# A stick-breaking attention loop: one copy moved from ScalarE to VectorE, four conditioning tiles and two column sums moved to later chunks

## The chip, the cores and the metric

The kernel runs on one NeuronCore of a Trainium2 chip. The metric is the device time of one execution in microseconds (us); lower is better.

## The reference, cut to what matters

Two layers with D_MODEL 2048, a sequence of 256 tokens, 16 heads of 128, and D_FF 8192. Layer 0 mixes tokens by stick-breaking attention, layer 1 by a short convolution; each is followed by a squared-ReLU MLP. Shift, scale and gate vectors come from a conditioning vector c through a product with mod_w, 2048 x 12288 per layer.

```python
mod = (cond @ mod_w[i] + mod_b[i])[:, None, :]
sh_m, sc_m, g_m, sh_f, sc_f, g_f = jnp.split(mod, N_MOD, axis=-1)
h = x * (1.0 + sc_m) + sh_m
# attention, each head:
z = jnp.einsum('bqhd,bkhd->bhqk', qb, kb) * scale
log_beta = jax.nn.log_sigmoid(z)
log_1m = jnp.where(causal, jax.nn.log_sigmoid(-z), 0.0)
log_stick = lax.cumsum(log_1m, axis=3, reverse=True) - log_1m
a = jnp.where(causal, jnp.exp(log_beta + log_stick), 0.0)
outs.append(jnp.einsum('bhqk,bkhd->bqhd', a, vb))
...
return o @ w_o
x = layer_norm(DEEPNORM_ALPHA * x + (1.0 + g_m) * y, ln_g[i, 0], ln_b[i, 0])
```

## The kernel before

**Weight products.** Each float32 operand is split into a rounded "high" part and the remainder, "low", and TensorE adds three products (high x high, high x low, low x high; L1215 to L1217). Weights go through in numbered chunks of 128 x 1024 elements. SyncE loads a chunk into one of eight places of `raw`; ScalarE writes `w_high` (L559), which has four slots; VectorE writes `w_low` (L872) and with it tells TensorE and the loader that the chunk is there and that its place is free. ScalarE may start on chunk n+4 when TensorE is through chunk n. So ScalarE's copy for chunk n+3 starts when chunk n begins on TensorE, where it isn't held up otherwise. A group is eight chunks, which fill two PSUM banks (128 tokens each). The chunks of the value projection are 64 to 95, those of the output projection W_O are 96 to 127; 96 to 99 are split before the attention loop.

**The conditioning vectors.** Their weights come as tiles of 128 x 1024. VectorE multiplies and adds each into `mod_acc` (L830; the first tile of a block of 16 is L827), through a ring of five buffers. When the 16 tiles of a block are done, TensorE sums over the partitions (`sum_mod`: eight transposes, L1241, or four matmuls for a gate, L1235) behind the chunk that SUMS_AFTER names, and VectorE takes the sums in (`write_block`, L838 and L861) in the step that WRITE_AFTER names. `step(n)` on VectorE is: `low(n)`, then a write if one is due, then the tiles of this step. All engine queues run in program order.

**The attention loop.** For head s: TensorE makes scores (L1350, L1352); ScalarE takes Abs, Exp and Ln (L630 to L634); VectorE makes the softplus (`sp`, L916); GpSimd masks it (L455, written to `stage`); TensorE adds running sums to the scores (`sums`, L1359 to L1361); ScalarE takes Exp (`probs`, L661); GpSimd masks that (L455); TensorE makes the output (L1371, L1373) in one of two PSUM tiles. Each engine's step s has a fixed order. TensorE: scores(s), sums(s-2), output(s-3). ScalarE: the three functions of head s, the Exp of head s-2, and `output_high(s-4)`, which copies a head's output to `h_high` (L652). VectorE: softplus(s), the tiles of this step, then the low part of output s-4 (L935). GpSimd: mask of softplus s, mask of probs s-2. TensorE's output(o) waits until the low part of output o-2 is written. The last two heads' sums and outputs run between the first chunks of W_O.

**The end of W_O.** `last_group` runs chunks 120 to 123 over both halves of the tokens, with a column sum behind a chunk where one is named, then chunks 124 to 127 over the first half, then the same four over the second. VectorE's part is this:

```python
                for j in range(SLOTS, NCH):
                    step(last + j)
                    if j == SLOTS:
                        take_both(n, NG - 2)
                take(n, NG - 1, 0)
```

Here `last` is 120; `take` adds a finished bank of the group to the residual rows (`take_both` both halves), and step 125 stands behind step 124 and `take_both`.

Of the kernel before, what the change touches and what calls it, by code (L numbers as in the profile page):

```python
# [23 lines left out]
ACT = mybir.ActivationFunctionType  # L24
# [4 lines left out]
CREDIT_BANKS = 2  # L29
# [5 lines left out]
def build_trunk(nc, x, c, mod_w, mod_b, ln_g, ln_b, attn_w_qkv, attn_w_o,  # L35
# [4 lines left out]
    KT = D // P  # L40
    TT = T // P
    HEADS = KT
    GC = 512
    GT = GC // P
    NCH = 8
# [13 lines left out]
    W_O = W_V + NG  # L59
# [19 lines left out]
    BANK0 = PARTS - 2 * NG  # L79
# [22 lines left out]
    def block_of(unit, half=HALVES - 1):  # L102
        return STARTS + HALVES * UNIT_ORDER.index(unit) + half
# [22 lines left out]
    N_V, N_O, N_HEADS, N_MLP0 = W_V * NCH, W_O * NCH, W_O * NCH + SLOTS, W_MLP[0] * NCH  # L126
# [4 lines left out]
    def start_chunk(p, jj):  # L131
        return LEADING * jj + p if p < LEADING else PART_CH * p + jj

    HEAD_TILES = {s: 1 for s in range(3, 16)} | {16: 2, 17: 2, 18: 2, 19: 1}
    N_HEAD_TILES = sum(HEAD_TILES.values())
    HEADS_BLOCK, HEADS_SUM, HEADS_WRITE = 8, 12, 14
    SUMS_AFTER = {12: 2, 27: 3, 42: 4, 58: 5, 74: 6, 90: 7, N_HEADS + 3: 9, N_HEADS + 20: 10}
    WRITE_AFTER = {14: 2, 30: 3, 45: 4, 62: 5, 78: 6, 94: 7, N_HEADS + 7: 9, N_HEADS + 24: 10}

    def tiles_early(n):  # L140
        if n < QC - 2:
            return 2 if n >= FIRST_STEP else 0
        if n < N_O:
            return 2 if n in (QC + 8, 2 * QC + 8) else 1
        return int(n < N_HEADS + 20)

    H_HIGH_ORDER = [(0, 0), (0, 1), (0, 2), (1, 0), (1, 1), (1, 2), (0, 3), (1, 3)]
    H_LOW_ORDER = [(0, 0), (0, 1), (1, 0), (0, 2), (1, 1), (1, 2), (0, 3), (1, 3)]
# [8 lines left out]
    done = TILES_FIRST + N_HEAD_TILES + sum(TILES_OF)  # L157
    for n0, n1, unit in ((N_MLP0 + 8, W_TAIL[1] * NCH + 20, UNITS + SHIFT_F),
                         (W_CIN * NCH + 8, W_COUT * NCH + 20, UNITS + SCALE_F),
                         (W_MLP[1] * NCH + 12, W_MLP[1] * NCH + 160, UNITS + GATE_F)):  # L160
        first, last, free = done, block_of(unit) * KT, 0
        TILES_OF += [0] * (n0 - len(TILES_OF))
        while done < last:
            n, now = len(TILES_OF), 0
            wanted = first + (n - n0 + 1) * (last - first) / (n1 - n0)
            while n >= free and done + now < min(wanted, last) and now < 2:
                now += 1
                if (done + now) % KT == 0:
                    SUMS_AFTER[n], WRITE_AFTER[n + 4], free = (done + now) // KT, (done + now) // KT, n + 4
            TILES_OF.append(now)  # L170
            done += now
    TILES_OF += [0] * (N_CHUNKS - len(TILES_OF))
# [14 lines left out]
    with ctx:  # L187
        def sb(name, shape, dt=F32):
            return ctx.enter_context(nc.sbuf_tensor(name, shape, dt))

        def sem(name):
            return ctx.enter_context(nc.semaphore(name))
# [15 lines left out]
        h_high = sb("h_high", [P, KT, T], F32R)  # L208
# [33 lines left out]
        o_ps = [bank[2][:, 0:T], bank[3][:, 0:T]]  # L242
# [18 lines left out]
        LEAD = 3  # L261
        STEPS = HEADS + 3
# [14 lines left out]
        banks_free = sem("banks_free")  # L277
# [23 lines left out]
        att_a, att_am, att_o = sem("att_a"), sem("att_am"), sem("att_o")  # L301
        att_hi, att_lo = sem("att_hi"), sem("att_lo")
# [196 lines left out]
        def _(act):  # L499
# [10 lines left out]
            for b, parts in enumerate(batches):  # L510
                row = 0 if b else KT
                for part in parts:
                    n = part.shape[0]
# [111 lines left out]
            def soft_log(s):  # L625
                e = soft[s % 2]
                act.wait_ge(att_z, s + 1)
                if s >= 2:
                    act.wait_ge(att_sp, s - 1)
                act.activation(e, z_ps[s % 4][:, 0:ZC], ACT.Abs).then_inc(att_act, 1)  # L630
                act.wait_ge(att_act, 2 * s + 1)
                act.activation(e, e, ACT.Exp, scale=-1.0).then_inc(att_act, 1)
                act.wait_ge(att_act, 2 * s + 2)
                act.activation(e, e, ACT.Ln, bias=1.0).then_inc(att_l, 1)  # L634
# [12 lines left out]
                    act.wait_ge(chunk_mult, W_O * NCH + CREDIT_SPLIT)  # L647
                empty(g % 2, lambda b: v_tok[:, b, g * GC:(g + 1) * GC])

            def output_high(o):  # L650
                act.wait_ge(att_o, o + 1)
                act.activation(h_high[:, o, :], o_ps[o % 2], ACT.Copy).then_inc(att_hi, 1)  # L652

            for s in range(2, HEADS + 2):
                if LEAD <= s < HEADS:
                    soft_log(s)
                a = s - 2
                act.wait_ge(att_cum, a + 1)
                if a >= 3:
                    act.wait_ge(att_o, a - 2)  # L660
                act.activation(probs[:, a % 3, :], z_ps[a % 4][:, 0:ZC], ACT.Exp).then_inc(att_a, 1)  # L661
                if s >= 4:
                    output_high(s - 4)
            for o in range(HEADS - 2, HEADS):
                output_high(o)

            def make_h(n, t, q):

# [121 lines left out]
        def _(dve):  # L790
# [79 lines left out]
            def low(n):  # L870
                dve.wait_ge(high_done, n + 1)
                dve.tensor_tensor(w_low[:, n % SLOTS], raw[:, n % NCH], w_high[:, n % SLOTS].bitcast(F32),  # L872
                                  ALU.subtract).then_inc(raw_used, 1)

            def step(n):

                low(n)
                if n in WRITE_AFTER:
                    write_block(WRITE_AFTER[n])
                add_tiles(TILE_AT[n], TILE_AT[n] + TILES_OF[n])  # L880
# [31 lines left out]
            def softplus(s):  # L912
                dve.wait_ge(att_l, s + 1)
                if s >= 3:
                    dve.wait_ge(att_cum, s - 2)
                dve.scalar_tensor_tensor(out=sp[s % 3], in0=z_ps[s % 4][:, 0:ZC], scalar=0.0,  # L916
                                         in1=soft[s % 2], op0=ALU.max, op1=ALU.add).then_inc(att_sp, 1)
# [3 lines left out]
            head_tile = TILE_AT[N_HEADS] - N_HEAD_TILES  # L921


            for s in range(LEAD, STEPS + 1):
                if s < HEADS:
                    softplus(s)
                if s == HEADS_WRITE:
                    write_block(HEADS_BLOCK)
                add_tiles(head_tile, head_tile + HEAD_TILES.get(s, 0))
                head_tile += HEAD_TILES.get(s, 0)  # L930
                o = s - 4
                if o < 0:
                    continue
                dve.wait_ge(att_hi, o + 1)
                dve.tensor_tensor(h_low[:, o, :], o_ps[o % 2], h_high[:, o, :].bitcast(F32),  # L935
                                  ALU.subtract).then_inc(att_lo, 1)
# [218 lines left out]
            n = LNS - 1  # L1155
# [17 lines left out]
        def _(pe):  # L1173
# [55 lines left out]
            def sum_mod(b):  # L1229

                pe.wait_ge(mod_chain, block_chained(b))
                acc = mod_acc[:, b % 2, :]
                if is_gate(b):
                    for i in range(2):
                        ins = pe.matmul(gate_ps[i][:, :], ones[:], acc[:, cols(i)], start=True, stop=True)  # L1235
                elif b > 1:
                    if b == 2:
                        pe.wait_ge(turned_out, 2 + TT * NG)
                    for t in range(WT):
                        dst = turned_sums(b)[t // GT][:, t % GT * P:(t % GT + 1) * P]  # L1240
                        ins = pe.transpose(dst, acc[:, t * P:(t + 1) * P], ident[:])  # L1241
                else:
                    for t in range(WT // 2):
                        ins = pe.matmul(mod_ps[:, t:t + 1], acc[:, t * P:(t + 1) * P], ones[:, 0:1],
                                        start=True, stop=True)
                ins.then_inc(mod_sums, 1)

            def sum_after(n):
                if n in SUMS_AFTER:
                    sum_mod(SUMS_AFTER[n])  # L1250

# [111 lines left out]

            def output(o):
                dst = o_ps[o % 2]
                if o == 0:
                    pe.wait_ge(banks_free, BANK0 + CREDIT_BANKS + W_O)
                pe.wait_ge(att_am, o + 1)
                if o >= 2:
                    pe.wait_ge(att_lo, o - 1)  # L1370
                pe.matmul(dst, v_tok[:, 0, o * P:(o + 1) * P], probs[:, o % 3, 0:T],  # L1371
                          start=True, stop=False, skip_group_check=True)
                pe.matmul(dst[:, P:T], v_tok[:, 1, o * P:(o + 1) * P], probs[:, o % 3, T:ZC],  # L1373
                          start=False, stop=True, skip_group_check=True).then_inc(att_o, 1)

            def heads(s):
                if LEAD <= s < HEADS:
                    scores(s)
                if 2 <= s < HEADS + 2:
                    sums(s - 2)  # L1380
                if s >= 3:
                    output(s - 3)
# [7 lines left out]
            for g in range(NG):  # L1390
                group(W_V + g, g % 2, h_high, h_low, None, lead_scores if g == NG - 1 else None, SLOTS - 1)

            for s in range(2, STEPS - 2):
                heads(s)
                if s == HEADS_SUM:
                    sum_mod(HEADS_BLOCK)
# [71 lines left out]
```

## Time and profile before

| | us |
|---|---|
| median of 3 runs | 2301.97 (2300.68 to 2302.37) |
| the profiled execution | 2302.37 |
| its span in the trace | 2300.6 |
| TensorE busy | 2236.2 (97% of the span) |
| VectorE busy | 1680.9 (73%) |
| ScalarE busy | 1142.9 (50%) |
| GpSimd busy | 32.1 (1%) |

The span is the part of the execution that the trace covers. Busy time is the union of an engine's instructions and says nothing of who waits for whom; the chain of work and the timeline do. The attention loop lies at about 329 to 371 us, the output projection behind it at 371 to 462 us.

### The profile page before, as it was taken

The page shows a single profiled execution, that of the slowest core. Times are in us where ns is not written, and L with a number is a line of the kernel's source. Part 1 is how long each engine was busy: PE and PEld are TensorE (multiplying, and loading weights), DVE is VectorE, ACT ScalarE, POOL GpSimd, SP SyncE. Part 2 cuts the span into 40 slices and gives each one's busy share as a digit, 9 for nine tenths or more (in the row PEclk, how much of TensorE's full clock was granted, in tenths as well). Part 3 has the DMA queues.
Part 4 walks back from the last instruction along what each step waited for, and adds up shares of the span by engine and source line. Part 5 has one row for each costly group of instructions (what it writes and reads, how often), then busy time and mean ns, then how long its engine had stood idle before and what let it go on. Part 6 is the DMA issues. An engine that isn't in the chain of part 4 may idle for free.

```text
span 2300.6 us, 27995 instructions
## 1 busy us (share of the span) xinstructions
PE 2236.2 (97%) x10862; PEld 1883.0 (82%) x10862; DVE 1680.9 (73%) x1683; ACT 1142.9 (50%) x1441; POOL 32.1 (1%) x55
## 2 busy tenths in 40 slices
PE   4999999999999999999999999999999999999997
PEld 4999877878888888888878888887888888888885
DVE  6898888887776777777778698877666565555556
ACT  2677455375345445445455444436634544543642
POOL 0000012000000000000000000000000000000000
PEclk9999999999999999999999999999999999999998
DMA  9999998779888888888849878866877667666662
GB/s 350 372 387 393 372 325 286 280 275 343 293 284 281 297 293 271 296 297 279 281 151 376 288 274 301 290 225 219 282 238 229 222 227 239 208 191 191 183 230 84
DMA packets 281523, 627.08 MB, mean 273 GB/s; under 512 B 19232, under 2 KB 27952, under 8 KB 279344
## 3 DMA queue, kind: packets, MB, share of 16 engines
q1 hardware_dynamic: 278432, 608.25, 77.4%
q10 hardware_dynamic: 2960, 17.05, 1.8%
q8 instruction: 87, 1.43, 0.3%
q14 instruction: 44, 0.36, 0.0%
HBM read 623.12 MB, written 2.10 MB: 272 GB/s over the span
## 4 chain that ended last, share of the span: by engine, by line
PE 91%; DVE 3%; DMA 3%; ACT 1%; issue 1%; POOL 1%; SPq 0%; DVEq 0%; ACTq 0%
PE bank L1215 28%; PE bank L1216 28%; PE bank L1217 27%; DMA mod_raw<-in_mod_w 3%; PE bank L1225 2%; PE bank L1205 2%; PE bank L1208 2%; PE bank L1207 2%; DVE mod_acc L830 1%; PE bank L1235 1%; PE bank L1241 1%; DVE w_low L872 0%; POOL stage L455 0%; ACT stage L677 0%; DVE mod_acc L818 0%
## 5 line engine op out<-in xcount | busy, mean ns | idle before, releaser
L872 DVE TENSOR_TENSOR w_low<-raw,w_high 128x1024 fp32r<-128x1024 f32 x768 | 936.1, 1223 | 539.0 <-ACT w_high L559 537.9
L559 ACT ACTIVATE w_high<-raw 128x1024 fp32r<-128x1024 f32 x768 | 810.3, 1059 | 1022.6 <-PE bank L1217 1012.6
L1215 PE MATMUL bank<-w_high,h_high 128*128 128x512 f32 x1664 | 656.4, 394 | 2.4 <-issue 1.4
L1217 PE MATMUL bank<-w_high,h_low 128*128 128x512 f32 x1664 | 648.8, 390 | 0.0
L1216 PE MATMUL bank<-w_low,h_high 128*128 128x512 f32 x1664 | 648.7, 390 | 0.0
L830 DVE SCALAR_TENSOR_TENSOR mod_acc<-mod_raw,cond,mod_acc 128x1024 f32<-128x1024 f32 x345 | 441.8, 1281 | 16.7 <-DMA mod_raw<-in_mod_w 14.2
L1215 PE MATMUL bank<-w_high,hid_high 128*128 128x512 f32 x1152 | 449.9, 391 | 0.0
L1217 PE MATMUL bank<-w_high,hid_low 128*128 128x512 f32 x1152 | 448.5, 389 | 0.0
L1216 PE MATMUL bank<-w_low,hid_high 128*128 128x512 f32 x1152 | 448.4, 389 | 0.0
L1215 PEld LDWEIGHTS bank<-w_high,h_high 128*128 128x128 f32 x1664 | 312.9, 188 | 70.6 <-issue 5.1
L1217 PEld LDWEIGHTS bank<-w_high,h_low 128*128 128x128 f32 x1664 | 312.8, 188 | 65.3
L1216 PEld LDWEIGHTS bank<-w_low,h_high 128*128 128x128 f32 x1664 | 313.1, 188 | 64.1 <-issue 1.4
L1217 PEld LDWEIGHTS bank<-w_high,hid_low 128*128 128x128 f32 x1152 | 216.3, 188 | 44.9
L1215 PEld LDWEIGHTS bank<-w_high,hid_high 128*128 128x128 f32 x1152 | 216.3, 188 | 44.7 <-issue 0.2
L1216 PEld LDWEIGHTS bank<-w_low,hid_high 128*128 128x128 f32 x1152 | 216.4, 188 | 44.5 <-issue 0.2
L1205 PE MATMUL bank<-h_high,w_high 128*128 128x256 f32 x512 | 148.7, 290 | 10.2 <-DVE w_low L872 7.2
L1207 PE MATMUL bank<-h_low,w_high 128*128 128x256 f32 x512 | 146.9, 287 | 0.0
L1208 PE MATMUL bank<-h_high,w_low 128*128 128x256 f32 x512 | 146.8, 287 | 0.0
L1205 PEld LDWEIGHTS bank<-h_high,w_high 128*128 128x128 f32 x512 | 100.4, 196 | 11.1 <-issue 8.0
L1207 PEld LDWEIGHTS bank<-h_low,w_high 128*128 128x128 f32 x512 | 100.4, 196 | 0.2 <-issue 0.2
L1208 PEld LDWEIGHTS bank<-h_high,w_low 128*128 128x128 f32 x512 | 100.3, 196 | 0.0
L746 ACT ACTIVATE stage<-bank,vec 128x256 f32<-128x256 f32 x128 | 49.6, 469 | 0.0
(118 smaller groups left out, 982.3 us busy)
## 6 DMA issues: line engine op xcount, KB each, us to landing
raw<-in_mlp_w SPq DMA_DIRECT2D x512, 512.0 KB, 4.5
mod_raw<-in_mod_w SPq DMA_DIRECT2D x368, 512.0 KB, 6.4
raw<-in_attn_w_qkv SPq DMA_DIRECT2D x96, 512.0 KB, 8.2
raw<-in_conv_w_in SPq DMA_DIRECT2D x96, 512.0 KB, 4.8
raw<-in_attn_w_o SPq DMA_DIRECT2D x32, 512.0 KB, 5.9
raw<-in_conv_w_out SPq DMA_DIRECT2D x32, 512.0 KB, 5.1
mod_raw<-in_mod_w SPq DMA_DIRECT2D x32, 256.0 KB, 7.4
gate_row<-in_mod_b ACTq DMA_DIRECT2D x4, 1024.0 KB, 7.5
```

The lines of the kernel that those rows point to most:

```text
L559: act.activation(w_high[:, n % SLOTS], raw[:, n % NCH], ACT.Copy).then_inc(high_done, 1)
L746: ins = act.activation(feat[:, m, :], bank[2 * (g % 2) + m // 2][:, T * (m % 2):T * (m % 2 + 1)], ACT.Relu, bias=vec[:, at:at + 1])
L830: dve.scalar_tensor_tensor(out=acc, in0=rows, scalar=cond[:, 1, k:k + 1], in1=acc, op0=ALU.mult, op1=ALU.add).then_inc(mod_chain, 1)
L872: dve.tensor_tensor(w_low[:, n % SLOTS], raw[:, n % NCH], w_high[:, n % SLOTS].bitcast(F32), ALU.subtract).then_inc(raw_used, 1)
L1205: pe.matmul(dst, wh[:, c], h_high[:, k, :], start=first and m % 2 == 0, stop=False, skip_group_check=True)
L1207: pe.matmul(dst, wh[:, c], h_low[:, k, :], start=False, stop=False, skip_group_check=True)
L1208: ins = pe.matmul(dst, wl[:, c], h_high[:, k, :], start=False, stop=last, skip_group_check=True)
L1215: pe.matmul(dst, high[:, k, c], wh, start=k == 0, stop=False, skip_group_check=True)
L1216: pe.matmul(dst, high[:, k, c], wl, start=False, stop=False, skip_group_check=True)
L1217: return pe.matmul(dst, low[:, k, c], wh, start=False, stop=k == KT - 1, skip_group_check=True)
L1225: ins = pe.transpose(bank[2 * par + m // 2][:, at:at + P], rows[:, t, m * P:(m + 1) * P], ident[:])
L1235: ins = pe.matmul(gate_ps[i][:, :], ones[:], acc[:, cols(i)], start=True, stop=True)
```

## The change

1. The copy of a head's output to `h_high` goes from ScalarE to VectorE. It stands there right behind the softplus, ahead of the tiles, for output s-3; its low part follows behind the tiles in the same step, so one step sooner than before.
2. The wait for the value projection's last banks stands ahead of the whole loop on TensorE instead of at output 0.
3. The loop takes 16 tiles instead of 20; steps 11 to 13 have none. The four others go to the chunks 100 to 121, which take 24 instead of 20: one each in chunks 100 to 107, none in 108 and 109, then 1, 1, 2 in turn.
4. The sum of block 9 moves from chunk 103 to 108 and its write from step 107 to 110. The sum of block 10 moves from behind chunk 120 to behind chunk 123; its write stays in step 124.
5. The other writes from the fifth block on come one step sooner (62, 78 and 94 become 61, 77 and 93; of the 13 later blocks each write comes three steps behind its sum instead of four).

```diff
-    HEAD_TILES = {s: 1 for s in range(3, 16)} | {16: 2, 17: 2, 18: 2, 19: 1}
+    HEAD_TILES = {s: 1 for s in range(3, 11)} | {14: 1, 15: 2, 16: 2, 17: 2, 18: 1}
-    SUMS_AFTER = {12: 2, 27: 3, 42: 4, 58: 5, 74: 6, 90: 7, N_HEADS + 3: 9, N_HEADS + 20: 10}
-    WRITE_AFTER = {14: 2, 30: 3, 45: 4, 62: 5, 78: 6, 94: 7, N_HEADS + 7: 9, N_HEADS + 24: 10}
+    SUMS_AFTER = {12: 2, 27: 3, 42: 4, 58: 5, 74: 6, 90: 7, N_HEADS + 8: 9, N_O + 3 * NCH + 3: 10}
+    WRITE_AFTER = {14: 2, 30: 3, 45: 4, 61: 5, 77: 6, 93: 7, N_HEADS + 10: 9, N_O + 3 * NCH + 4: 10}
...
-        return int(n < N_HEADS + 20)
+        if n < N_HEADS + 8:
+            return 1
+        if n < N_HEADS + 10:
+            return 0
+        return (1, 1, 2)[(n - N_HEADS - 10) % 3] if n < N_HEADS + 22 else 0
...
-                    SUMS_AFTER[n], WRITE_AFTER[n + 4], free = (done + now) // KT, (done + now) // KT, n + 4
+                    SUMS_AFTER[n], WRITE_AFTER[n + 3], free = (done + now) // KT, (done + now) // KT, n + 3
...
-            def output_high(o):
-                act.wait_ge(att_o, o + 1)
-                act.activation(h_high[:, o, :], o_ps[o % 2], ACT.Copy).then_inc(att_hi, 1)
...
-                if s >= 4:
-                    output_high(s - 4)
-            for o in range(HEADS - 2, HEADS):
-                output_high(o)
...
-            for s in range(LEAD, STEPS + 1):
+            for s in range(LEAD, STEPS):
                 if s < HEADS:
                     softplus(s)
+                o = s - 3
+                dve.wait_ge(att_o, o + 1)
+                dve.tensor_copy(h_high[:, o, :], o_ps[o % 2]).then_inc(att_hi, 1)
                 if s == HEADS_WRITE:
                     write_block(HEADS_BLOCK)
                 add_tiles(head_tile, head_tile + HEAD_TILES.get(s, 0))
                 head_tile += HEAD_TILES.get(s, 0)
-                o = s - 4
-                if o < 0:
-                    continue
                 dve.wait_ge(att_hi, o + 1)
...
             def output(o):
                 dst = o_ps[o % 2]
-                if o == 0:
-                    pe.wait_ge(banks_free, BANK0 + CREDIT_BANKS + W_O)
...
+            pe.wait_ge(banks_free, BANK0 + CREDIT_BANKS + W_O)
             for s in range(2, STEPS - 2):
                 heads(s)
```

N_O is 96, N_HEADS 100, NCH 8, LEAD 3, STEPS 19.

## Rows read from the trace of the kernel before

**Rows 1.** The page: GB/s moved in 40 slices; the last chain by engine.
```profile
GB/s 350 372 387 393 372 325 286 280 275 343 293 284 281 297 293 271 296 297 279 281 151 376 288 274 301 290 225 219 282 238 229 222 227 239 208 191 191 183 230 84
...
PE 91%; DVE 3%; DMA 3%; ACT 1%; issue 1%; POOL 1%; SPq 0%; DVEq 0%; ACTq 0%
```
**Rows 2.** Windows, W_O: busy per engine (PE, PEld, DVE, ACT, POOL), clock, DMA share, GB/s.
```profile
381.00:393.00 12.00, 12.00 (x55) 9.94 (x54) 12.00 (x12) 4.84 (x6) 0.00 (x0) 1.00 0.88 305
```
**Rows 3.** The chain in order of time (start, us, what): two steps, later a sum.
```profile
338.57 0.70 PE bank L1371 x2
...
341.82 0.57 DVE stage L916
...
342.45 1.39 POOL stage L455
...
344.25 0.70 PE bank L1371 x2
...
395.30 0.87 PE bank L1241 x8
```
**Rows 4.** Timeline of GpSimd (start, us, what; in brackets idle before, releaser).
```profile
365.13 0.41 POOL L455 TENSOR_SCALAR_AFFINE_SELECT stage<-stage 128x256 f32<-128x256 f32 x1 [0.86 <-DVE stage L916]
365.49 0.41 POOL L455 TENSOR_SCALAR_AFFINE_SELECT probs<-probs 128x256 f32<-128x256 f32 x1
...
369.88 0.40 POOL L455 TENSOR_SCALAR_AFFINE_SELECT probs<-probs 128x256 f32<-128x256 f32 x1
```
**Rows 5.** Timeline of VectorE in the attention loop.
```profile
342.29 1.28 DVE L830 SCALAR_TENSOR_TENSOR mod_acc<-mod_raw,cond,mod_acc 128x1024 f32<-128x1024 f32 x1
...
364.98 1.28 DVE L838 TENSOR_REDUCE sums<-bank 128x4 f32<-128x512 f32 x2
...
369.57 0.42 DVE L935 TENSOR_TENSOR h_low<-bank,h_high 128x256 fp32r<-128x256 f32 x1
369.91 1.45 DVE L830 SCALAR_TENSOR_TENSOR mod_acc<-mod_raw,cond,mod_acc 128x1024 f32<-128x1024 f32 x1
```
**Rows 6.** Timeline of ScalarE, at the loop's start.
```profile
330.45 0.58 ACT L618 ACTIVATE v_tok<-bank 128x512 f32<-128x512 f32 x1
```
**Rows 7.** Timeline of TensorE: first sums, outputs 0, 3 and 13.
```profile
328.75 0.59 PE L1359 MATMUL bank<-stage,neg_tri 128*128 128x256 f32 x2
...
332.93 0.67 PE L1371 MATMUL bank<-probs,v_tok 128*128 128x256 f32 x2 [1.61 <-POOL probs L455]
...
341.04 0.70 PE L1371 MATMUL bank<-probs,v_tok 128*128 128x256 f32 x2
...
370.33 0.70 PE L1371 MATMUL bank<-probs,v_tok 128*128 128x256 f32 x2 [0.42 <-POOL probs L455]
```
**Rows 8.** Timeline of VectorE in W_O: steps 100, 104, 105, then 124 to 126.
```profile
380.51 1.22 DVE L872 TENSOR_TENSOR w_low<-raw,w_high 128x1024 fp32r<-128x1024 f32 x1
381.65 1.28 DVE L830 SCALAR_TENSOR_TENSOR mod_acc<-mod_raw,cond,mod_acc 128x1024 f32<-128x1024 f32 x1
...
390.97 0.75 DVE L827 TENSOR_SCALAR mod_acc<-mod_raw,cond 128x1024 f32<-128x1024 f32 x1
391.63 1.22 DVE L872 TENSOR_TENSOR w_low<-raw,w_high 128x1024 fp32r<-128x1024 f32 x1
...
443.65 1.23 DVE L872 TENSOR_TENSOR w_low<-raw,w_high 128x1024 fp32r<-128x1024 f32 x1 [1.52 <-ACT w_high L559]
444.79 1.28 DVE L838 TENSOR_REDUCE sums<-bank 128x4 f32<-128x512 f32 x2
...
446.19 0.69 DVE L947 SCALAR_TENSOR_TENSOR gated<-gate_row,bank 128x512 f32<-128x512 f32 x1
...
450.30 2.35 DVE L872 TENSOR_TENSOR w_low<-raw,w_high 128x1024 fp32r<-128x1024 f32 x2
```
**Rows 9.** Timeline of ScalarE: `w_high` of chunks 103 and 127.
```profile
384.52 1.06 ACT L559 ACTIVATE w_high<-raw 128x1024 fp32r<-128x1024 f32 x1 [1.66 <-PE bank L1217]
...
451.58 1.06 ACT L559 ACTIVATE w_high<-raw 128x1024 fp32r<-128x1024 f32 x1 [1.66 <-PE bank L1217]
```

## The prediction, as made before the result was known

> **What bounds the kernel now.** I read the page first. The chain that ended last is TensorE for 91% of the span, and its clock is full (1.00, the 2.4 GHz level) where I looked [rows 1, 2]. So time is gained only where TensorE stands still, and lost wherever it is made to. Then I read the chain in order of time. In the attention loop it goes round one loop for two heads: output(o), scores(o+4), three functions on ScalarE, softplus on VectorE, two masks on GpSimd, output(o+2), 338.57 to 344.25, or 5.68 us [rows 3]. The softplus starts 3.25 us after the output; 0.63 us later GpSimd begins a mask that takes 1.39 us. Elsewhere the same mask takes 0.41 us [rows 4]. The timeline tells why: beside the long one VectorE runs a tile of 1.28 us, which started 0.15 us ahead of it and ended 0.27 us before the mask did [rows 3, 5]. Beside the 0.41 us masks VectorE read PSUM (L838, 364.98). A mask that started 0.03 us ahead of a tile (369.88, 369.91) took 0.40 us [rows 4, 5]. So a tile that starts first holds GpSimd, and work from PSUM does not. The other heads don't set the pace: from output 2 to output 3 is 2.47 us (338.57, 341.04), which is TensorE's own work of a step [rows 3, 7].
>
> In the output projection both TensorE and VectorE were busy for 12.00 of 12.00 us [rows 2]. A chunk takes TensorE (451.58 - 384.52 - 2 x 0.87) / 24 = 2.72 us, the 0.87 being a column sum [rows 3, 9]. On VectorE a low part costs 1.14 us (380.51 to 381.65), a block's first tile 0.66, and another tile 1.19, from five steps in 11.12 us; a write costs 1.40 (444.79 to 446.19), and `take_both` 4.11 (446.19 to 450.30) [rows 8]. VectorE started on chunk 100 at 380.51 and TensorE at 384.52, a lead of 4.0 us [rows 8, 9].
>
> **Part 1, the copy and the loop.** ScalarE loses 16 copies; it does not set the pace (each soft function follows TensorE), so that is worth nothing by itself. VectorE gets 16 copies of 128x256 from PSUM. No row shows one. The nearest is the low part of the same shape, also from PSUM: 0.42 us, next start 0.34 us behind it [rows 5]; I take 0.34, with 0 and 0.69 (twice) as bounds. The low part's own cover is the idle of VectorE in a step of 2.8 us.
>
> The copy pushes the tile back by 0.34 us, so the first mask now runs free beside work from PSUM. But the second mask, of probs, cannot start before softplus + 0.63 + 0.36 = 0.99 us [rows 3, 4], and the tile starts at 0.47 + 0.34 = 0.81 us. The tile is first by 0.18 us and holds the second mask until 0.27 us after its end. The cycle becomes 3.25 + 0.81 + 1.28 + 0.27 + 0.05 = 5.66 us against 5.68: nothing. In the other heads the copy must wait for its output, the tile comes after both masks, and TensorE's 2.47 us are the limit.
>
> The Trainium skill has a rule for this spacing (VectorE: DVE Perf Modes, "The DRAIN you can't avoid"): the next VectorE operation does not start until the pipe is empty. By it the copy would cost its full 0.42 us, the tile would still be first, by 0.10 us, and the sum would stay as it is; the row shows the next start 0.08 us before the end.
>
> The start: TensorE now waits for the value banks before sums(0). They are out at 331.03 (330.45 + 0.58) [rows 6], where sums(0) ran at 328.75 [rows 7]. Sums(0), scores(3) and sums(1) take two steps of TensorE without outputs, about 2.6 us, so output 0 starts at 333.64 instead of 332.93 [rows 7]. Softplus(3) is later by 1.5 us (Abs waits for scores(3) and the first Exp), so heads 1, 3, 5 become the slow ones. Walking on: output 1 at 336.84, 3 at 342.49, 5 at 348.14, 7 at 353.79; from there no tiles are in the way and TensorE's 2.47 us hold: output 9 at 358.73, 10 at 362.07 (with the sum of block 8, 0.87), 12 at 367.01. Softplus(14) starts at 365.32; behind it come copy, write of block 8 (1.40), a first tile (0.66) and a low part (0.34), so softplus(15) starts at 368.53. Its first tile, at 369.34, again beats the second mask: output 13 at 369.34 + 1.28 + 0.27 + 0.05 = 370.94, against 370.33 [rows 7]. What steps 11 to 13 gain goes at both ends. **Loop: +0.6 us.** The lead at chunk 100 becomes 3.6 us: VectorE's last copy waits for output 15, at 379.6, then copy, tile and low part (0.34 + 1.19 + 0.34) end at 381.5; TensorE is there at 385.1.
>
> **Part 2, chunks 100 to 123.** Steps 100 to 107 have a tile each; 108 and 109 none; `take_both` is in step 108. VectorE has low(110) written at about 407.7. Now it waits for the sum of block 9, behind chunk 108 on TensorE: 385.12 + 9 x 2.72 + 0.87 = 410.5. Everything behind the write waits with it, 2.8 us. Then write and first tile: step 111 at 412.6, and with 2.33 us for a step of one tile and 3.52 for two: 112 at 414.9, 113 at 418.4, 114 at 420.8, 115 at 423.1, 116 at 426.6. Step 116 has `take_both`: 117 at 433.1, its low part ready at 434.3. TensorE wants chunk 117 at 410.5 + 8 x 2.72 = 432.2, so it stands for 2.1 us; the two tiles of step 118 cost another 0.4, those of 121 come just in time. **+2.5 us.** Bounds: 0 if VectorE has 2.5 us more in hand; 2.8 more is the whole wait.
>
> **Part 3, chunk 124.** This is the largest term. The write of block 10 is in step 124, its sum now behind chunk 123. VectorE reaches step 124 some 6.8 us before TensorE is through chunk 123 (ScalarE's chunk 124 may start when chunk 121 does; two copies take 2.3 us; three chunks and a sum take 9.0), and stands there. When the sum is done TensorE begins the first half of chunk 124, 1.36 us, and then wants low(125). VectorE has ahead of that the write 1.40, `take_both` 4.11 and the low part 1.22 [rows 8]: 6.73 us, with 0.1 us for signals. TensorE stands for 6.83 - 1.36 = 5.5 us. Before, the sum was behind chunk 120 and low(125) ready at 451.5 (450.30 + 1.22), just ahead of 451.58 when chunk 124 began [rows 8, 9]. Low(126) and low(127) come every 1.2 us and are in time. Behind this is the layer norm, which waits for the half group: nothing takes the delay up. **+5.5 us.**
>
> **Part 4, the other writes.** A write three steps behind its sum makes VectorE wait up to about 1.3 us (2.72 + 0.87 - 1.06 - 1.23); TensorE's next need is three chunks off (8.2 us), and VectorE then has at most write, tile, `take_both` and a low part, 7.9 us. In steps 77 and 93 it waits up to 1.8 us, within the 4 us of lead. **0**, at worst 1 us.
>
> **Sum:** 0.6 + 2.5 + 5.5 = 8.6 us on the profiled execution's 2302.37 (span 2300.6): 2311.0. Against the median, 2301.97, that is 0.4 us less.
>
> **The rivals.**
> - *The masks escape (18%).* The margin of 0.18 us is small. If the second mask starts first, every step runs at TensorE's 2.47 us: output 9 at 333.64 + 9 x 2.47 = 355.87, output 13 at about 367.1 (softplus(15) 365.7), 3.8 us earlier than in my walk. Time: 2307.1, and 2304.6 if there is no stall of part 2. What would do it: a copy over 0.52 us long. The Trainium skill (SBUF — State Buffer, "Who interferes with whom") says that the shared port goes whole to whichever starts first, and that a VectorE operation with two SBUF inputs contends with a GpSimd one that reads SBUF; by that rule a mask in front would hold the tile instead, with the same 2307.1; the rows fit it.
> - *The wait at chunk 124 is hidden, not slower (8%).* Were VectorE still behind by 6.7 us or more in useful work when the sum of block 10 is done, its wait would be nothing. Then 2302.4 + 0.6 + 2.5 = 2305.5, within 0.2%. It decides from where the sum's end is less than 5.5 us before low(125) is wanted. Against it: VectorE's own list ends long before.
> - *Tiles come late (12%).* Chunks 110 to 121 ask for 28 transfers of 0.524 MB in 32.6 us, 450 GB/s, where the best slice had 393 [rows 1]: 4.7 us short. VectorE's wait at step 110 and the ring give part back; 2 to 3 us more: 2313.5.
> - *Only the loop's gain counts (3%).* Stalls of parts 2 and 3 absent and the masks escape: 2299.2, faster but within 0.2%.
>
> **How the numbers follow.** My case has 55%: 2311, its own range 2308.5 to 2312.5. 0.2% is 4.6 us, about what a measurement of this kernel can tell from no change; slower by it means over 2306.6. That is my case, late tiles, and two thirds of the first rival: 0.79. Within it: the rest of that rival, the hidden wait and most of the last, 0.17. Faster 0.04, left for what I have not seen. The range that holds 8 in 10 is 2305 to 2313.5, from the masks without part 2's stall to late tiles.
>
> **What would show it.** The wait of chunk 125's first product for w_low, 5.5 us, in TensorE's list; VectorE idle some 7 us before L838 in step 124; a wait of 2 us at chunk 117; in the loop masks of probs of 1.2 us and of softplus of 0.4 us at odd heads; output 0 at 333.6, output 13 at 370.9. I am wrong if low(125) is ready when chunk 124's half ends, or if all masks are short.

## The result and the profile after

The changed kernel took 2316.24 us (median of 4 runs, 2315.3 to 2316.73), the kernel before beside it 2301.32 us (4 runs): 14.9 us more, a ratio of 1.007 (95% interval 1.0058 to 1.0082). The sign was forecast, the size was not: the sum gave 8.6 us, and 2316.2 lies above the range's upper end of 2313.5. The profiled execution took 2318.76 us with a span of 2316.9, 16.3 us more than the span before; it is one of the longer ones of the 21 executions on record, which lie between 2315.3 and 2319.98 us.

TensorE's list of waits, 320 to 500 us (engine and line waited for, us in total, times, longest), has the waits that the prediction named; a wait of TensorE is called a stand here:

```profile
PE bank L1211 <- DVE w_low L868: 8.3, 3, 5.5
PE bank L1365 <- POOL probs L459: 6.0, 5, 2.4
PE bank L1355 <- ACT v_tok L622: 2.2, 1, 2.2
```

Its timeline places them: the first sums, output 13, chunk 117, the sum of block 10 and chunk 125. These rows answer to [rows 7]:

```profile
332.43 0.77 PE L1355 MATMUL bank<-stage,neg_tri 128*128 128x256 f32 x2 [2.18 <-ACT v_tok L622]
...
373.10 0.70 PE L1365 MATMUL bank<-probs,v_tok 128*128 128x256 f32 x2 [2.38 <-POOL probs L459]
...
438.47 0.54 PE L1211 MATMUL bank<-w_high,h_high 128*128 128x512 f32 x1 [2.55 <-DVE w_low L868]
...
459.24 1.03 PE L1237 MATMUL bank<-ident,mod_acc 128*128 128x128 f32 x8
...
467.17 0.77 PE L1211 MATMUL bank<-w_high,h_high 128*128 128x512 f32 x1 [5.53 <-DVE w_low L868]
```

The last stand is the forecast 5.5 us to within 0.1. VectorE's timeline shows why, and the wait for block 9 as well; these rows answer to [rows 8]. It idled 2.73 us ahead of the write in step 110, and 5.28 us in step 124 (I had said 2.8 and 6.8):

```profile
414.18 1.29 DVE L834 TENSOR_REDUCE sums<-bank 128x4 f32<-128x512 f32 x2 [2.73 <-PE bank L1237]
...
460.31 1.29 DVE L834 TENSOR_REDUCE sums<-bank 128x4 f32<-128x512 f32 x2 [5.28 <-PE bank L1237]
461.63 0.17 DVE L857 TENSOR_TENSOR mod<-sums,vec 128x8 f32<-128x8 f32 x1
461.72 0.69 DVE L943 SCALAR_TENSOR_TENSOR gated<-gate_row,bank 128x512 f32<-128x512 f32 x1
...
465.82 3.48 DVE L868 TENSOR_TENSOR w_low<-raw,w_high 128x1024 fp32r<-128x1024 f32 x3
```

What the sum did not have stands in the windows (PE, PEld, DVE, ACT and POOL busy, then the granted clock, the DMA share and GB/s). Behind each of the four stands the granted clock is 0.50, the level of 1.2 GHz, while TensorE is busy all the time:

```profile
333.00:336.30 3.30, 3.30 (x13) 2.94 (x12) 1.59 (x2) 1.39 (x3) 0.41 (x1) 0.50 0.97 359
373.90:377.30 3.40, 3.40 (x11) 2.63 (x10) 3.30 (x5) 0.00 (x0) 0.55 (x1) 0.50 0.85 253
438.70:442.10 3.40, 3.40 (x9) 2.66 (x9) 3.30 (x4) 0.00 (x0) 0.00 (x0) 0.50 0.84 260
467.20:472.90 5.70, 5.70 (x14) 4.44 (x15) 2.10 (x2) 0.00 (x0) 0.00 (x0) 0.50 0.80 273
```

Half of each such stretch is lost to the products in it: 1.65, 1.7, 1.7 and 2.85 us, together 7.9. Not all of that reaches the end, as a run below shows. The mean granted clock of the whole execution tells the same for the executions without a profile: it is 0.991 or 0.992 in all 21 of the changed kernel, and 0.993 to 0.996 in the 68 of the kernel before that ran beside the experiments; 0.003 of 2316 us is 7 us.

The time lost can be read at ScalarE's copies for chunks 103, 122 and 128, which are released by TensorE's chunks; here for the kernel before, which [rows 9] has at chunk 103 with 384.52:

```profile
437.09 1.06 ACT L559 ACTIVATE w_high<-raw 128x1024 fp32r<-128x1024 f32 x1 [1.66 <-PE bank L1217]
...
458.38 1.06 ACT L559 ACTIVATE w_high<-raw 128x1024 fp32r<-128x1024 f32 x1 [5.74 <-PE bank L1217]
```

and for the changed kernel, with chunk 92 first (307.08 before), at the end of the part that the change barely touches:

```profile
308.42 1.06 ACT L563 ACTIVATE w_high<-raw 128x1024 fp32r<-128x1024 f32 x1 [0.69 <-PE bank L1213]
...
388.88 1.06 ACT L563 ACTIVATE w_high<-raw 128x1024 fp32r<-128x1024 f32 x1 [1.66 <-PE bank L1213]
...
445.89 1.06 ACT L563 ACTIVATE w_high<-raw 128x1024 fp32r<-128x1024 f32 x1 [1.68 <-PE bank L1213]
...
475.64 1.06 ACT L563 ACTIVATE w_high<-raw 128x1024 fp32r<-128x1024 f32 x1 [15.08 <-PE bank L1213]
```

The differences are 1.3, 4.4, 8.8 and 17.3 us. So the loop and the first chunks of W_O cost 3.0 us (forecast 0.6), chunks 100 to 118 another 4.4 (2.5), chunk 124 and behind it 8.5 (5.5). Then 1.0 us comes back: the profile of the kernel before has a stretch at 0.50 behind its third layer norm and the changed kernel's has none there. The row before:

```profile
1565.10:1568.50 3.40, 3.31 (x8) 2.67 (x9) 3.24 (x6) 3.34 (x11) 0.00 (x0) 0.50 0.31 81
```

The 1.3 us ahead of chunk 92 belong to these two executions: that difference was there by chunk 24, ahead of anything that the change moves, and in the profiles of the experiments it lies between -2.0 and +1.7 us. It is about what the 16.3 us between the spans have over the 14.9 between the medians.

### The profile page after: what moved, and what is told of

Same layout as the page of the kernel before. It is cut to its first block, busy times and chain, and to the rows that moved or that the text cites. A ratio compares the mean times of both kernels' runs of the same rounds, so it can differ in the third digit from the quotient of the medians.

```text
span 2316.9 us, 27995 instructions
## 1 busy us (share of the span) xinstructions
PE 2242.1 (97%) x10862; PEld 1886.3 (81%) x10862; DVE 1686.0 (73%) x1699; ACT 1138.9 (49%) x1425; POOL 26.9 (1%) x55
## 4 chain that ended last, share of the span: by engine, by line
PE 91%; DVE 3%; DMA 3%; ACT 1%; issue 1%; POOL 0%; SPq 0%; DVEq 0%; ACTq 0%
PE bank L1211 27%; PE bank L1212 27%; PE bank L1213 27%; DMA mod_raw<-in_mod_w 3%; PE bank L1221 2%; PE bank L1201 2%; PE bank L1203 2%; PE bank L1204 2%; DVE mod_acc L826 1%; PE bank L1231 1%; PE bank L1237 1%; DVE w_low L868 1%; ACT stage L673 0%; POOL probs L459 0%; DVE mod_acc L814 0%
```

## The experiments

Two theories stood behind the first four runs. Theory A: a stand costs its own length and then what the fallen clock takes. Theory B: a stand costs its length alone, and the other 6 us come from somewhere else. Each kernel ran against the kernel before on the same chip.

**The sum of block 10 alone.** The kernel before with

```diff
-    SUMS_AFTER = {..., N_HEADS + 3: 9, N_HEADS + 20: 10}
+    SUMS_AFTER = {..., N_HEADS + 3: 9, N_O + 3 * NCH + 3: 10}
```

> The kernel before, with one edit: the sum of block 10 behind chunk 123 instead of 120. Theory A (the stand of TensorE at chunk 124 costs its own length, 5.5 us, and then the clock that has fallen behind it costs about 2.9 us more): 8.4 us slower than before, with granted clock 0.50 in a stretch behind the stand. Theory B (a stand costs only its length; the rest of the 14.9 us comes from elsewhere): 5.5 us slower. If the sum's place doesn't matter: 0.

Measured: 2308.82 against 2301.31 us, 7.5 us slower, ratio 1.0031 (1.0020 to 1.0043). Its profile has the same stand and the same clock behind it (timeline of TensorE, then the window):

```profile
457.70 0.77 PE L1215 MATMUL bank<-w_high,h_high 128*128 128x512 f32 x1 [5.53 <-DVE w_low L872]
```
```profile
454.70:461.50 6.80, 3.80 (x9) 3.06 (x10) 5.05 (x6) 0.00 (x0) 0.00 (x0) 0.50 0.42 131
```

Here the clock fell 3 us ahead of the stand's end, and only the 3.8 us behind it (461.50 - 457.70) count: 5.5 + 1.9 = 7.4 us. The interval, 4.6 to 9.9 us, holds both theories' numbers; it is the profile, where chunks 122 to 128 took 7.6 us longer than before at a clock of 0.50 behind the stand, that speaks for A. One number in a schedule is half of the loss.

**TensorE kept busy at chunk 124.** The changed kernel, with 20 products in the stand:

```diff
                     ins = chunk(w, par, j, (0,), high, low)
+                    if w == W_O + NG - 1 and j == SLOTS:
+                        for _ in range(20):
+                            pe.matmul(bank[5][:, :], high[:, 0, 0:P], w_high[:, 0, 0, :], start=True, stop=True,
+                                      skip_group_check=True)
```

> The changed kernel, with 20 matrix products of 128x512 that nobody reads put behind the first half of chunk 124 (4.5 us of TensorE's time at full clock), so that TensorE works while VectorE is late. Theory A (fallen clock): the 4.5 us disappear in the wait of 5.5 us, the clock stays at 1.00 behind it, and the time falls by 2 to 3 us, to some 12 us over the kernel before. Theory B: no change, 14.9 us over before. If the stand is shorter than thought: slower by up to 4.5 us.

Measured: 2313.87 us against 2301.31, ratio 1.0052 (1.0039 to 1.0064): 2.4 us less than the changed kernel's median with more work on TensorE. Its profile has no stretch at 0.50 behind chunk 124, and from chunk 127 to 128 it is 2.6 us shorter. The median alone would not decide it, since the two intervals overlap; the clock in the trace does.

**The sum of block 10 at chunk 121.**

```diff
-    SUMS_AFTER = {..., N_HEADS + 8: 9, N_O + 3 * NCH + 3: 10}
+    SUMS_AFTER = {..., N_HEADS + 8: 9, N_O + 3 * NCH + 1: 10}
```

> The changed kernel, with the sum of block 10 behind chunk 121 instead of 123 (its last tile is in step 121); the write stays in step 124. Theory A: stand and fallen clock at chunk 124 both gone, 8.4 us less than the changed kernel, 6.5 us over before. Theory B: 5.5 us less, 9.4 us over before. Either way a wait of up to 1 us may be left, for the sum or for the low part of chunk 125.

Measured: 2309.62 us, 1.0034 (1.0021 to 1.0046), 8.3 us over before and 6.6 under the changed kernel. That lies between A (6.5 over) and B (9.4), and nearer to B. The profile says where A's number went: the stand of 5.5 us is gone, and chunks 122 to 128 cost 0.7 us over before instead of 8.5; but a stretch at 0.50 turned up later, at 472.6 us behind the layer norm, where TensorE stands for 1.7 us in this version as before, and took about 1.1 us again.

**The copy alone.** The kernel before with the copy on VectorE (the edits to `output_high` and to the loop on VectorE as in the change), tiles as

```diff
-    HEAD_TILES = {s: 1 for s in range(3, 16)} | {16: 2, 17: 2, 18: 2, 19: 1}
+    HEAD_TILES = {s: 1 for s in range(3, 15)} | {15: 2, 16: 2, 17: 2, 18: 2}
```

> The kernel before with the copy on VectorE alone: 20 tiles in the loop (one in steps 3 to 14, two in 15 to 18), the wait for the value banks at output 0, sums and writes as before. My walk through the loop (the tile still starts ahead of the second mask; two heads in 5.66 us): 0 us, within 1.5. If the masks escape: 3 us faster. If the copy on VectorE is on the path: 16 x 0.34 = 5.4 us slower.

Measured: 2304.89 us, 1.0013 (1.0004 to 1.0022): 3.6 us slower, outside the 1.5 that I allowed. Up to chunk 103 it lost 0.7 us, as the walk would have it; then 1.0 us at chunk 117, where VectorE's low part came late (it began chunk 100 only 2.3 us ahead of TensorE, where it had 4.0), and 1.5 us in a stretch at 0.50 behind the first layer norm that the profile of the kernel before doesn't have. TensorE stood for 2.67 us ahead of output 13 here, and the clock stayed at 1.00 behind it.

**The early wait undone.** The changed kernel with

```diff
             def output(o):
                 dst = o_ps[o % 2]
+                if o == 0:
+                    pe.wait_ge(banks_free, BANK0 + CREDIT_BANKS + W_O)
...
-            pe.wait_ge(banks_free, BANK0 + CREDIT_BANKS + W_O)
             for s in range(2, STEPS - 2):
```

> The changed kernel, with the wait for the value banks back at output 0. My walk: output 0 is 0.7 us earlier and the loop ends 0.6 us earlier. Theory A (fallen clock): the stand of 2.2 us ahead of the first sums is gone and with it the stretch at 0.50 behind it, 1.7 us more; in all 2.3 us less than the changed kernel, 12.6 us over before. Theory B: 0.7 us less, 14.2 over before.

Measured: 2313.35 against 2301.44 us, 1.0055 (1.0043 to 1.0068): 2.9 us less than the changed kernel. No stand and no fallen clock at the loop's start. A's 2.3 is nearer than B's 0.7, but the intervals of the two kernels overlap widely. The profile agrees with A's sum: from chunk 92 to 103 it is 2.4 us shorter than the changed kernel's. The split is less sure: the run with the sum of block 10 behind chunk 121 has the stand and no fall behind it, and is 1.1 us shorter there; so the fall is about 1.1 of the 2.4, and the stand 1.3.

**The low part ahead of the tiles.** The changed kernel, with the wait at output 0, the sum of block 10 behind chunk 121, and

```diff
+                dve.wait_ge(att_hi, o + 1)
+                dve.tensor_tensor(h_low[:, o, :], ...)
                 if s == HEADS_WRITE:
                     write_block(HEADS_BLOCK)
                 add_tiles(head_tile, head_tile + HEAD_TILES.get(s, 0))
                 head_tile += HEAD_TILES.get(s, 0)
-                dve.wait_ge(att_hi, o + 1)
-                dve.tensor_tensor(h_low[:, o, :], ...)
```

> The changed kernel with the low part of each output ahead of the step's tiles, the wait for the value banks at output 0 and the sum of block 10 behind chunk 121. The tile then starts 0.47 + 0.34 + 0.45 = 1.26 us behind the softplus, behind both masks (0.99). If the masks set the loop's pace: all masks 0.4 us, 2.47 us a step, output 13 some 4 us earlier than before; with the stand at chunk 117 and its fallen clock (4.2 us) left and 0.7 us at chunk 125, about 1 us over before. If VectorE's own work sets the pace: no gain in the loop, 5 us over before.

Measured: 2301.43 against 2301.44 us, 1.0001 (0.9992 to 1.0010). The masks set the pace: chunk 103's copy came 5.1 us sooner than before (0.3 of it was there at chunk 92), and the stand at chunk 117 took 4.4 us of it away again.

**The sum of block 9 at chunk 107.**

```diff
-    SUMS_AFTER = {..., N_HEADS + 8: 9, ...}
-    WRITE_AFTER = {..., N_HEADS + 10: 9, ...}
+    SUMS_AFTER = {..., N_HEADS + 7: 9, ...}
+    WRITE_AFTER = {..., N_HEADS + 11: 9, ...}
```

> The changed kernel with the sum of block 9 behind chunk 107 and its write in step 111 (108 and 110 in the changed kernel). If VectorE's wait for this sum makes TensorE stand at chunk 117: VectorE no longer waits 2.7 us, the stand of 2.5 us is gone or under 0.5 us, and the 1.7 us of fallen clock with it; 4 us less than the changed kernel, 11 us over before. If the tiles (24 instead of 20) or their transfers are to blame: no change.

Measured: 2314.56 us, 1.0059 (1.0045 to 1.0073), 1.7 us less than the changed kernel where 4 were expected; its five runs lie between 2309.93 and 2315.93, wider than any other's. The mechanism is shown: VectorE no longer waits in that place, and the stand at chunk 117 is gone; there are 0.32 us at chunk 119, where the prediction had 0.4 for the two tiles of step 118 (VectorE, then TensorE):

```profile
408.23 1.22 DVE L868 TENSOR_TENSOR w_low<-raw,w_high 128x1024 fp32r<-128x1024 f32 x1
409.37 1.28 DVE L834 TENSOR_REDUCE sums<-bank 128x4 f32<-128x512 f32 x2
```
```profile
437.90 0.47 PE L1211 MATMUL bank<-w_high,h_high 128*128 128x512 f32 x1 [0.32 <-DVE w_low L868]
```

The profiled execution is the shortest of the five, and the only one with a mean granted clock of 0.994; the other four have 0.991 or 0.992 and take 2312.98 to 2315.93 us. So how much the stand's removal saves is not settled. This profile also taught that a stand does not always bring the clock down: TensorE stood 2.18 us ahead of the first sums and 2.37 us ahead of output 13, as in the changed kernel, and the clock stayed at 1.00 behind both (timeline, then the window, of the first):

```profile
331.38 0.70 PE L1355 MATMUL bank<-stage,neg_tri 128*128 128x256 f32 x2 [2.18 <-ACT v_tok L622]
```
```profile
333.00:336.30 3.30, 3.30 (x22) 2.92 (x20) 2.00 (x4) 2.76 (x7) 1.52 (x3) 1.00 0.92 282
```

**A version with four tiles ahead of the loop.** The kernel before with the copy on VectorE, the low part ahead of the tiles, and

```diff
-    HEAD_TILES = {s: 1 for s in range(3, 16)} | {16: 2, 17: 2, 18: 2, 19: 1}
+    HEAD_TILES = {s: 1 for s in range(3, 14)} | {15: 1, 16: 1, 17: 2, 18: 1}
...
-            return 2 if n in (QC + 8, 2 * QC + 8) else 1
+            return 2 if n in (QC + 8, 2 * QC + 8, 76, 80, 84, 88) else 1
```

> The kernel before with the copy on VectorE and the low part ahead of the tiles; 16 tiles in the loop (steps 3 to 13 one, 14 none, then 1, 1, 2, 1), the other four in chunks 76, 80, 84 and 88, where VectorE idles 0.3 us a chunk; sums, writes, the chunks from 96 on and the wait at output 0 as before. If the tile that holds the second or first mask sets the loop's pace: 2.47 us a step, about 3.8 us faster than before. If the four tiles don't fit ahead of the loop, up to 3 us of this are lost.

Measured: 2297.62 against 2301.44 us, 0.9983 (0.9974 to 0.9991): 3.8 us faster, as worked out. That the number is met is in part luck: in the profile the loop gained 5.1 us (chunk 92 to 103), not 3.8, and 1.5 us went again up to chunk 136, with a stretch at 0.50 behind the first layer norm. The mechanism holds: from 333 to 364 us every mask takes 0.41 us, and most softplus come 2.45 us apart; GpSimd's timeline, and VectorE's (L921 is the copy, L923 the low part, L822 the tile), which answer to [rows 4, 5]:

```profile
338.83 0.41 POOL L455 TENSOR_SCALAR_AFFINE_SELECT stage<-stage 128x256 f32<-128x256 f32 x1 [1.68 <-DVE stage L908]
339.19 0.41 POOL L455 TENSOR_SCALAR_AFFINE_SELECT probs<-probs 128x256 f32<-128x256 f32 x1
```
```profile
338.21 0.55 DVE L908 SCALAR_TENSOR_TENSOR stage<-bank,stage 128x384 f32<-128x384 f32 x1
338.68 0.41 DVE L921 CAST h_high<-bank 128x256 fp32r<-128x256 f32 x1
339.13 0.42 DVE L923 TENSOR_TENSOR h_low<-bank,h_high 128x256 fp32r<-128x256 f32 x1
339.47 1.28 DVE L822 SCALAR_TENSOR_TENSOR mod_acc<-mod_raw,cond,mod_acc 128x1024 f32<-128x1024 f32 x1
340.66 0.55 DVE L908 SCALAR_TENSOR_TENSOR stage<-bank,stage 128x384 f32<-128x384 f32 x1
```

**All four stands kept busy.** The changed kernel with `fill`, which issues products of 128x512 into a bank that is free there:

```diff
+            def fill(b, k):
+                for _ in range(k):
+                    pe.matmul(bank[b][:, :], h_high[:, 8, 0:P], h_high[:, 8:10, :], start=True, stop=True,
+                              skip_group_check=True)
...
+            fill(1, 8)
             pe.wait_ge(banks_free, BANK0 + CREDIT_BANKS + W_O)
...
+                if s == HEADS:
+                    fill(0, 8)
                 if s >= 3:
                     output(s - 3)
...
+                    if w == W_O + 2 and j == 5:
+                        fill(5, 9)
                     chunk(w, par, j, range(TT), high, low).then_inc(chunk_mult, 1)
...
                     ins = chunk(w, par, j, (0,), high, low)
+                    if w == W_O + NG - 1 and j == SLOTS:
+                        fill(5, 20)
```

The four calls stand ahead of the wait for the value banks, ahead of output 13, ahead of chunk 117 and behind the first half of chunk 124.

> The changed kernel with matrix products of 128x512 that nobody reads in all four stands of TensorE: 8 ahead of the wait for the value banks, 8 ahead of output 13, 9 ahead of chunk 117, 20 behind the first half of chunk 124; each batch is shorter than its stand. The stands keep their length. Theory A (fallen clock, four stretches that cost 1.6, 1.7, 1.7 and 2.9 us): no stretch at 0.50 between 330 and 480 us and up to 7.9 us less than the changed kernel, 7 to 9 us over before, near the 8.6 us of the prediction's sum. Theory B: no change, 14.9 us over before.

Measured: 2310.36 against 2301.57 us, 1.0041 (1.0028 to 1.0053), 8.8 us over before and 5.9 under the changed kernel, and the two intervals don't meet. One window over all of it has the clock at 1.00:

```profile
330.00:480.00 150.00, 141.21 (x699) 117.77 (x698) 129.63 (x172) 68.66 (x112) 18.74 (x33) 1.00 0.72 249
```

The same dependencies with a busy TensorE cost 8.8 us; the other 6 us are the clock. The prediction's sum, which knows only the dependencies, was 8.6. That it comes so near is in part luck: by the copies for chunks 92, 103, 123 and 128 (305.10, 382.81, 441.52 and 466.15 us here; 307.08, 384.52, 439.81 and 458.38 before) this profile lost 0.3, 3.4 and 6.1 us, 9.7 in all, and about 1 us came back because it has no stretch at 0.50 behind the third layer norm.

**Busy behind the layer norms.** The faster version with, in `tail`,

```diff
                 if n < LNS - 1:
+                    pe.wait_ge(banks_free, w0 + NG + BANK0 + 1)
+                    fill(0, 7)
                     turn_xn(n, 0)
```

> The version with the low part ahead of the tiles (3.8 us faster than before), and 7 unread products ahead of the first turned rows behind each of the first three layer norms, where TensorE stands for 1.7 us and in this version's profile two of three stands had a stretch at 0.50 behind them. Theory A: those stretches go, up to 1.5 us each: 5 to 7 us faster than before. Theory B: no change, 3.8 us faster; if the products outlast the stand: less than that.

Measured: 2300.27 against 2301.57 us, 0.9995 (0.9985 to 1.0004): 2.5 us of the gain lost. The products stood ahead of the first turned quarter, which doesn't wait, and so pushed back what ScalarE makes of the rows; TensorE then stood at the first chunk instead. I moved them between the third and the fourth quarter:

```diff
                     i = (n * TT + t) * NG + q
+                    if t == 0 and q == NG - 1:
+                        pe.wait_ge(banks_free, W_TAIL[n] + NG + BANK0 + 1)
+                        fill(0, 6)
                     pe.wait_ge(xn_done, i + 1)
```

> As the version with the low part ahead of the tiles (3.8 us faster than before), and 6 unread products right inside the stand of 1.7 us behind each of the first three layer norms, between the third and the fourth turned quarter; in the version before this one they stood ahead of the first quarter, which does not wait, and pushed the rows back. Theory A: no row is pushed back, the stretches at 0.50 behind these stands go, 5 to 7 us faster than before. Theory B: 3.8 us faster, as without them.

Measured: 2296.25 against 2300.89 us, 0.9978 (0.9969 to 0.9987), 4.6 us faster than before, and the fastest version of all. Its profile has no stretch at 0.50 between 54 and 2282 us. Against the version without the products (0.9974 to 0.9991) the gain is inside the intervals, so that the products help is not shown.

## Why the prediction was wrong

**The step that failed** is the price of a stand: part 3 has "TensorE stands for 6.83 - 1.36 = 5.5 us" and then "nothing takes the delay up. **+5.5 us.**", and part 2 and the loop are priced in the same way, by the length of the wait alone. A stand also risks the clock of what runs behind it, and that cost 6 us of the 14.9 here. I had read the clock only where it was full [rows 2] and put its fall at nothing, in the sum and in the rivals. The Trainium skill says the clock is gated by how busy the array has been (TensorE: Matmul & The Clock Gate, "Part 1: The HAM clock gate"); the trace agrees, with 0.50 behind all four stands of 2.2 to 5.5 us. The terms, forecast, measured, and measured with TensorE kept busy in the stands:

| | forecast | profile | kept busy |
|---|---|---|---|
| loop and first chunks of W_O | 0.6 | 3.0 | 0.3 |
| chunks 100 to 119 | 2.5 | 4.4 | 3.4 |
| chunk 124 | 5.5 | 8.5 | 6.1 |

The last two columns differ by 2.7, 1.0 and 2.4 us, together 6.2; the four stretches are worth 7.9. In the loop the first stretch's 1.65 us reach output 13 only in part: it came at 373.10 against 370.33 [rows 7]. That is 2.8 us later; 1.3 of them were there ahead of chunk 92, which leaves 1.4, where 0.6 was forecast. The rest of the 3.0 is the stretch behind it.

**Part 1 was right, down to the order on the port.** The copy took 0.41 us, the tile came 0.34 us behind it and ahead of the second mask, so in every second head up to head 7 the mask of probs took 1.39 us and that of softplus 0.41, and two heads took 5.68 us again, from 343.31 to 348.99 (VectorE, then GpSimd):

```profile
343.15 0.41 DVE L925 CAST h_high<-bank 128x256 fp32r<-128x256 f32 x1
343.49 1.30 DVE L826 SCALAR_TENSOR_TENSOR mod_acc<-mod_raw,cond,mod_acc 128x1024 f32<-128x1024 f32 x1
```
```profile
343.31 0.41 POOL L459 TENSOR_SCALAR_AFFINE_SELECT stage<-stage 128x256 f32<-128x256 f32 x1 [2.17 <-DVE stage L912]
343.67 1.39 POOL L459 TENSOR_SCALAR_AFFINE_SELECT probs<-probs 128x256 f32<-128x256 f32 x1
```

The rival that the masks escape did not come true here. It did where the low part stood between copy and tile; there it was worth 5.1 us in the loop, more than the 3.8 that I had worked out for it. What the Trainium skill says of the port (SBUF — State Buffer, "Who interferes with whom"), that the first to start has it, fits both: the mask 0.18 us behind the tile took 1.39 us, and those ahead of it 0.41.

**Part 2:** the wait of 2.7 us for block 9's sum (2.8 forecast) made the stand at chunk 117, 2.55 us where I had 2.1; the one at chunk 119, 0.4, did not come, since TensorE was at half speed meanwhile; with the clock at 1.00 it came, 0.40 us long. The run with the sum at chunk 107 shows the cause. **Part 3:** 5.53 us, and alone it is 7.5 of the loss. The idle of VectorE was 5.3 and not 6.8 us, since it came to step 124 later than I had it; the wait ended with the same sum, so this changes nothing. **Part 4:** right, no wait of TensorE behind 500 us is longer than before. The transfers of the tiles were not late: VectorE's list of waits from 380 to 462 us has the two sums (8.0 us) and one output (2.2 us), and none for a tile.

## What to carry to other kernels

Where one engine bounds a kernel, a wait that is put on its helper must be followed to the first instruction queued behind it: a write that waits for a later sum held a low part that had nothing to do with it, and one such number cost 7.5 us. Price a stand of TensorE as its length plus a chance that up to half the length of the stretch behind it is lost, and look at the granted clock behind every stand in the trace before, not only where the engine is busy. Where GpSimd works beside VectorE, order VectorE's queue so that work from PSUM runs beside GpSimd's and the operations with two SBUF inputs come behind it.

## What was not expected of the hardware

Stands of 2.2 to 2.6 us were enough to bring TensorE's clock to 0.50, but not each time. Over all profiles the 2.18 us ahead of the first sums had 0.50 behind them in two and 1.00 in two; the 2.4 to 2.7 us ahead of output 13 had 0.50 in four and 1.00 in two; the 2.5 us at chunk 117 and the 5.5 us at chunk 125 had 0.50 each time, five and four times. And the stand of 1.7 us behind the layer norms had 0.50 behind it in one place out of three in the kernel before, in two in the faster version and in none in the changed kernel. So executions of one kernel can differ by such stretches: the five with the sum at chunk 107 have mean clocks of 0.991 to 0.994 and lie 6.0 us apart. Whether the place of a stand in time decides it was not tried.
